# Four schedule edits to a two-block transformer kernel: squares one pair later, rotations by exchanged rows, first squares added by GpSimd, a second bank for odd heads

## The chip, the cores and the metric

One core of one Trainium2 chip runs the whole program in one launch. The metric is the device time of that core in microseconds; the number quoted for a kernel is the median of its runs.

## The reference, cut to what matters

256 tokens of 2048 features pass through two blocks of two layers each, all in float32. The first block has a sparse and a latent attention mixer, each followed by a 4096-wide gated feed-forward; the second has two "hybrid" layers with four groups of four heads (fox, diff, moba, gla).

```python
x = x + rms_norm(mixer(rms_norm(x, g1)), g2)          # layers 0 and 1 of the first block
x = x + rms_norm(channel_mixer(rms_norm(x, g3)), g4)
...
q1, q2, k1, k2 = (partial_rope(t, *rope_diff) for t in (q1, q2, k1, k2))
mq = partial_rope(to_heads(p["moba_q"], HEAD_DIM), *rope_moba)
mk = partial_rope(to_heads(p["moba_k"], HEAD_DIM), *rope_moba)
...
def partial_rope(t, cos, sin):                        # half = 8 rows (diff) or 16 (moba)
    t1, t2, rest = t[..., :half], t[..., half:rot], t[..., rot:]
    return jnp.concatenate([t1 * c - t2 * s, t1 * s + t2 * c, rest], axis=-1)
```

## The kernel before

Features lie on the 128 partitions and tokens along the row, so a tile is 128 x 256 and the state `X` has 16 tiles. The weights stream from HBM in 902 units of eight 128 x 128 blocks (512 KB). SyncE loads a unit into one of four `RING` buffers. ScalarE copies it rounded to fp32r (`high`, L882, into `WHI`), VectorE subtracts to get the remainder (`low`, L1296, into `WLO`), and TensorE multiplies: each block costs three 256-column products, or one of 512 and one of 256 columns in the wide form. A unit's `low` lets SyncE load the next one, and `unit_used` from TensorE frees its `WHI`/`WLO` pair, four deep. Every engine runs its own instruction stream in order and meets the others at semaphores; the four streams are written out from one schedule.

The work beside the weight products (attention heads, rotations, norms, gates) is written as generators. `later(n, part)` starts a part at the n-th unit of a stage, `together` runs several in the order in which they are listed, and each engine advances them by one step for each unit (`tick`). The steps of one engine at one tick follow that tick's `high` or `low`.

A normalised product begins with a `lead`: four outputs are accumulated at once over 16 tiles of `X`, two tiles (a pair) for each unit. For each pair ScalarE writes the rounded `H` tile (`halve`, L897) and the squares (`square`, L889), VectorE writes the remainder (L1306), and TensorE adds the squares over the partitions with a product by a table of ones into bank 7 (`square_sums`, L525). There are five leads. The first waits for the table (`TB`) that ScalarE's queue loads with the inputs; `square` waits until TensorE has read the buffer four tiles back (`sq_read`). In the other four, VectorE first makes the new `X` tile (L1348 and L1350), from the norm of the branch before.

Where an output run ends in a norm, GpSimd adds the squares of 15 tiles (`sums`, L1998 and L2001), and TensorE makes two products: one of that sum (L531) and one of the last square (L533). ScalarE's last square stands behind the `high` copies of that step.

A hybrid layer has 29 tiles of projections (58 units, ticks 0 to 57), values (32 units, ticks 58 to 89) and gates. The rotation of a tile is a TensorE product with a 128 x 128 table (L679, bank 5), three VectorE operations (L1687 to L1689), 16 tiles for each layer, one at a tick from tick 48 and from tick 59. A head passes over its iterations: scores (L830), masks and maxima, exponentials (L1234), normalising (L1885), transposes (L840), the product with the values (L820, L821) into `head_bank`, always bank 7, and VectorE's copy out of it (L1894, `p_head_taken`), which the next head's product waits for. GLA's values product (`gla_heads`, L787 and L789, banks 4 and 5) comes at tick 74 on TensorE; fox's last copy is at tick 73 on VectorE.

Of the kernel before, what the change touches and what calls it, by code (L numbers as in the profile page):

```python
# [14 lines left out]
P = 128  # L15
T = 256
KT = 16
# [4 lines left out]
BANKS = 4  # L22
# [13 lines left out]
       ("moba_cos", 256), ("moba_sin", 256), ("diff_rot", 128), ("moba_rot", 128), ("mla_rot", 128),  # L36
# [49 lines left out]
def program(nc, xT, pos, w, vec, tab, out, n_units):  # L86
# [3 lines left out]
    with ctx:  # L90
# [120 lines left out]
        class Heads:  # L211


            def __init__(self, kind):
# [3 lines left out]
                self.split = kind in ("dsa", "mla")  # L218
                if kind == "mla":
# [41 lines left out]
        def head_bank(h):  # L261
            return BANK[7][:, 0:T]
# [25 lines left out]
        def pooled(k):  # L288
# [13 lines left out]
        ROPE_DIFF, ROPE_MOBA = [[(at + h, f"{kind}_rot", tcol(f"{kind}_cos", T), tcol(f"{kind}_sin", T))  # L302
                                 for at in tiles for h in range(4)]
                                for kind, tiles in (("diff", (Z_DQ, Z_DK)), ("moba", (Z_MQ, Z_MK)))]
# [94 lines left out]
        SUMMED_ADDED = (1, 3, 5, 7, 9, 10)  # L399
# [46 lines left out]
        def _(pe):  # L446
            c = {}
# [70 lines left out]
            def square_sums(tiles):  # L518

                if tiles[0] == 0:  # L520
                    step_no(c, "event")
                    pe.wait_ge(sem("tables"), 16)
# [272 lines left out]
            def heads(kind, l, p0, v0):  # L795
# [15 lines left out]
                for k in range(a.n + 2):  # L811
                    if k >= 2:
# [7 lines left out]
                        mm(head_bank(h), a.value(0, h), p[:, 0:T], start=True, stop=False)  # L820
                        mm(head_bank(h)[:, P:T], a.value(1, h), p[:, T:T + P], start=False, stop=True)\  # L821
# [28 lines left out]
            def hybrid(l):  # L850
# [3 lines left out]
                    later(48, rope(ROPE_DIFF)), later(59, rope(ROPE_MOBA)),  # L854
# [16 lines left out]
        def _(act):  # L871
# [27 lines left out]
            def first_norm():  # L899
# [5 lines left out]
                act.dma_start(TB[:, :], tab).then_inc(sem("tables"), 16)  # L905
                act.dma_start(V[:, KT:], vec[:, KT:]).then_inc(sem("vectors"), 16)
# [13 lines left out]
            def lead(r, u0):  # L920
                (name, l), e = c["lead"], step_no(c, "lead_event") - 1
                x0 = step_no(c, "x_new", KT) - KT if u0 else 0
                for p in range(UB):
# [10 lines left out]
                    for k in (2 * p, 2 * p + 1):  # L934
                        square(k, X[:, k, :], "sq_read", e)
                    if p >= 2:
                        high(u0 + SPLIT + p - 2, 0, 0)
                        tick(c)
                high(u0 + SPLIT + 6, 0, 0)
                tick(c)  # L940
                if u0 == 0:
# [1256 lines left out]
```

## Time and profile before

| | us |
|---|---|
| median of 3 runs | 2869.17 (2868.96 to 2871.13) |
| the profiled execution, time | 2871.13 |
| its span, first to last instruction | 2869.3 |
| TensorE busy | 2775.5 (97%) |
| VectorE busy | 1946.3 (68%) |
| ScalarE busy | 1382.3 (48%) |
| GpSimd busy | 505.5 (18%) |

The profiled execution is 1.96 us above the median of the runs; some 2 us of its time lie outside its span. TensorE's products overlap in the records, so its busy share is not the share of its peak. A wait of another engine counts for the time only where TensorE ends up waiting too.

### The profile page before, as it was taken

Reading aid. Unit: us, or ns where it says so; the run is one execution under the profiler, and the core shown is the slowest. Engines: PE = TensorE matmul, PEld = TensorE weight load, DVE = VectorE, ACT = ScalarE, POOL = GpSimd, SP = SyncE. Lnnn points to the kernel's source line nnn. Section 1 sums busy time; section 2 is a strip of 40 time slices with the busy share of each in tenths; the row PEclk is TensorE's granted clock in tenths of the full one; section 3 lists DMA queues with packets and bytes.
Section 4 is the critical chain, followed back from the end, with each engine's and each line's share of the span. In section 5 each row is a group of like instructions: output and inputs, shape, how many; then the busy total and the mean of one; then the engine's idle time right before and its main releaser. Section 6 shows DMA issues by size and latency. Waiting matters only on the chain.

```text
span 2869.3 us, 50364 instructions
## 1 busy us (share of the span) xinstructions
PE 2775.5 (97%) x18406; PEld 2504.2 (87%) x18406; DVE 1946.3 (68%) x2829; ACT 1382.3 (48%) x1931; POOL 505.5 (18%) x472
## 2 busy tenths in 40 slices
PE   8999999999999999989999999999999999999998
PEld 8998888888888899888888888899878889987887
DVE  4585568777754687668777754586767766676775
ACT  4434555544544447445554543453346454334553
POOL 0060034444411000022444421000000010000001
PEclk9999999999999999999999999999999999999999
DMA  6555445555555454444555555455444555444454
GB/s 226 165 165 184 138 141 181 186 185 185 183 191 184 145 172 156 132 147 147 190 187 184 185 190 184 152 165 162 159 148 150 167 184 169 162 155 153 147 170 139
DMA packets 131914, 481.71 MB, mean 168 GB/s; under 512 B 14768, under 2 KB 14896, under 8 KB 131632
## 3 DMA queue, kind: packets, MB, share of 16 engines
q1 hardware_dynamic: 130608, 475.06, 50.7%
q10 hardware_dynamic: 1152, 4.47, 0.4%
q8 instruction: 112, 1.84, 0.3%
q14 instruction: 42, 0.34, 0.0%
HBM read 477.38 MB, written 2.10 MB: 167 GB/s over the span
## 4 chain that ended last, share of the span: by engine, by line
PE 88%; DVE 6%; ACT 3%; POOL 2%; issue 1%; DMA 1%; ACTq 0%; DVEq 0%; POOLq 0%
PE BANK L458 32%; PE BANK L453 26%; PE BANK L459 16%; PE BANK L474 7%; DVE WLO L1296 2%; ACT WHI L882 1%; PE BANK L525 1%; PE BANK L830 1%; PE BANK L820 1%; PE BANK L465 1%; DMA TB<-tab 1%; PE BANK L679 0%; DVE TM L1885 0%; POOL M L2014 0%; DVE TM L1318 0%
## 5 line engine op out<-in xcount | busy, mean ns | idle before, releaser
L1296 DVE TENSOR_TENSOR WLO<-RING,WHI 128x1024 fp32r<-128x1024 f32 x902 | 1109.5, 1232 | 676.9 <-ACT WHI L882 670.7
L882 ACT ACTIVATE WHI<-RING 128x1024 fp32r<-128x1024 f32 x902 | 953.2, 1058 | 1152.3 <-PE BANK L459 641.1
L458 PE MATMUL BANK<-H,WHI 128*128 128x512 f32 x2560 | 918.7, 403 | 15.1 <-DVE H L1306 10.1
L453 PE MATMUL BANK<-H,WHI 128*128 128x256 f32 x4160 | 772.3, 288 | 22.8 <-DVE H L1306 19.5
L459 PE MATMUL BANK<-H,WLO 128*128 128x256 f32 x2560 | 720.4, 281 | 0.0
L453 PEld LDWEIGHTS BANK<-H,WHI 128*128 128x128 f32 x4160 | 656.8, 193 | 30.6 <-issue 23.8
L458 PEld LDWEIGHTS BANK<-H,WHI 128*128 128x128 f32 x2560 | 483.9, 189 | 136.9 <-issue 16.0
L453 PE MATMUL BANK<-H,WLO 128*128 128x256 f32 x2080 | 591.5, 284 | 0.0
L458 PE MATMUL BANK<-BIGR,WHI 128*128 128x512 f32 x1536 | 541.5, 398 | 3.5 <-DVE BIGR L1913 3.5
L459 PEld LDWEIGHTS BANK<-H,WLO 128*128 128x128 f32 x2560 | 486.2, 190 | 1.7 <-issue 1.0
L459 PE MATMUL BANK<-BIGR,WLO 128*128 128x256 f32 x1536 | 431.1, 281 | 0.0
L453 PEld LDWEIGHTS BANK<-H,WLO 128*128 128x128 f32 x2080 | 402.0, 193 | 0.0
L458 PEld LDWEIGHTS BANK<-BIGR,WHI 128*128 128x128 f32 x1536 | 288.4, 188 | 74.7 <-DVE BIGR L1913 4.2
L459 PEld LDWEIGHTS BANK<-BIGR,WLO 128*128 128x128 f32 x1536 | 290.2, 189 | 0.0
L474 PE MATMUL BANK<-WHI,H 128*128 128x512 f32 x640 | 213.6, 403 | 1.7 <-DVE BIG L1394 1.7
L2001 POOL TENSOR_TENSOR TM<-TM 128x256 f32<-128x256 f32 x84 | 114.3, 1360 | 421.4 <-ACT TM L1000 415.6
L1967 POOL TENSOR_TENSOR TM<-TM,RS 128x256 f32<-128x256 f32 x128 | 116.7, 914 | 361.8 <-DVE TM L1301 360.2
L1998 POOL COPY TM<-TM 128x256 f32<-128x256 f32 x6 | 5.9, 978 | 946.9 <-ACT TM L1000 638.7
L453 PE MATMUL BANK<-BIGR,WHI 128*128 128x256 f32 x688 | 135.2, 295 | 11.5 <-DVE BIGR L1680 4.0
L474 PEld LDWEIGHTS BANK<-WHI,H 128*128 128x128 f32 x640 | 120.2, 188 | 27.4 <-DVE BIG L1394 2.3
L1301 DVE TENSOR_REDUCE TM<-BANK 128x256 f32<-128x512 f32 x128 | 87.8, 690 | 63.1 <-PE BANK L459 63.1
L474 PE MATMUL BANK<-WLO,H 128*128 128x512 f32 x320 | 124.8, 390 | 0.0
(280 smaller groups left out, 2392.5 us busy)
## 6 DMA issues: line engine op xcount, KB each, us to landing
RING<-w SPq DMA_DIRECT2D x902, 512.0 KB, 3.3
X<-xT ACTq DMA_DIRECT2D x4, 512.0 KB, 10.0
TB<-tab ACTq DMA_DIRECT2D x1, 1536.5 KB, 16.7
outT<-M SPq DMA_DIRECT2D x3, 512.0 KB, 2.9
V<-vec ACTq DMA_DIRECT2D x1, 644.0 KB, 19.0
outT<-M SPq DMA_DIRECT2D x2, 256.0 KB, 3.2
BIG<-pos ACTq DMA_DIRECT2D x1, 128.0 KB, 3.9
V<-vec ACTq DMA_DIRECT2D x1, 8.0 KB, 6.9
```

The lines of the kernel that those rows point to most:

```text
L453: last = mm(bank[:, 0:T], wt[s][:, kk, :], x, start=start and n == 0, stop=stop and n == 2)
L458: mm(bank[:, :], WHI[s][:, kk, :], both, start=start, stop=False)
L459: return mm(bank[:, 0:T], WLO[s][:, kk, :], hi, start=False, stop=stop)
L465: last = mm(pair[t][:, 0:T], x[:, t * P:(t + 1) * P], wt[s][:, kk:kk + 2, :].rearrange("p a b -> p (a b)"), start=start and n == 0, stop=s ...
L474: last = mm(pair[t][:, :], x[:, t * P:(t + 1) * P], wt[s][:, kk:kk + 4, :].rearrange("p a b -> p (a b)"), start=start and n == 0, stop=sto ...
L525: last = mm(BANK[7][:, 0:T], ones, TM[:, k % 4, :], start=k == 0, stop=k == KT - 1)
L820: mm(head_bank(h), a.value(0, h), p[:, 0:T], start=True, stop=False)
L882: A(WHI[at % SPLIT][:, :, :], RING[at % RAW][:, :].rearrange("p (k n) -> p k n", k=UB), ACT.Copy)\
L1296: TT(WLO[at % SPLIT][:, :, :], RING[at % RAW][:, :].rearrange("p (k n) -> p k n", k=UB), WHI[at % SPLIT][:, :, :].bitcast(f32), ALU.subtra ...
L1301: return v.tensor_reduce(dst, bank[:, :].rearrange("p (a t) -> p t a", a=2), AX.X, ALU.add)
L1967: g.tensor_tensor(y, y, RS[:, :], ALU.mult).then_inc(sem("y_scaled"), 1)
L2001: g.tensor_tensor(TM[:, 4, :], TM[:, 4, :], TM[:, k % 4, :], ALU.add).then_inc(sem("sq_added"), 1)
```

## The change

1. In every lead, ScalarE squares the pair before the one that it has just halved, and the last pair after the loop. VectorE moves the remainder of tile k-1 between the two operations that make tile k of `X`.
2. In the first lead TensorE makes no product of single squares; GpSimd adds them (`sums`), and TensorE makes two products at the lead's end. The first 384 columns of the table go out after the second quarter of `X`; the rest, with the parameters, goes out at the fifth pair, and ScalarE and VectorE wait for them at the end of that run.
3. At the last step of a run that ends in a norm, the square goes ahead of the last `high`.
4. Rotations use no product: twelve transfers for each hybrid layer copy the partner rows of four tiles at once into `TM[8:12]` (four for each of the two diff turns, two for each of the two moba turns), and VectorE makes three operations of 1024 columns for four tiles, one at a tick. The sign has gone into the sine table, and two 128-column tables are gone.
5. Odd heads of dsa, mla and fox use bank 5, so that a head waits for the copy of the head before the last. GLA's values product waits for fox's four copies.

```diff
+    self.banks = 2 if kind in ("dsa", "mla", "fox") else 1
-        def head_bank(h):
-            return BANK[7][:, 0:T]
+        def head_bank(a, h):
+            return BANK[5 if a.banks == 2 and h % 2 else 7][:, 0:T]
...
-        SUMMED_ADDED = (1, 3, 5, 7, 9, 10)
+        SUMMED_ADDED = (0, 1, 3, 5, 7, 9, 10)
... TensorE, lead
-                    if h:
+                    if h and u0:
                         square_sums((2 * h - 2, 2 * h - 1))
-                square_sums((KT - 2, KT - 1))
+                if u0:
+                    square_sums((KT - 2, KT - 1))
+                else:
+                    pe.wait_ge(sem("ones"), 16)
+                    sums()
... TensorE, gla_heads and heads
+                pe.wait_ge(sem("p_head_taken"), HEADS_1 + 12 * l + 4)
-                        if h0 + h >= 1:
-                            pe.wait_ge(sem("p_head_taken"), h0 + h)
+                        free = h0 + h + 1 - (a.banks if h else 1)
+                        if free:
+                            pe.wait_ge(sem("p_head_taken"), free)
... TensorE, hybrid
-                    later(48, rope(ROPE_DIFF)), later(59, rope(ROPE_MOBA)),
... ScalarE, lead
-                    for k in (2 * p, 2 * p + 1):
-                        square(k, X[:, k, :], "sq_read", e)
+                    for k in (2 * p - 2, 2 * p - 1) if p else ():
+                        square(k, X[:, k, :], taken, e)
+                    if u0 == 0 and p == 4:
+                        act.dma_start(TB[:, TO["chunk"]:], tab[:, TO["chunk"]:]).then_inc(sem("tables"), 16)
+                        act.dma_start(V[:, KT:], vec[:, KT:]).then_inc(sem("vectors"), 16)
... ScalarE, the last step of a run that ends in a norm
-                    early = upo if r.kind in ("m", "add") or taps_led else upo - 1
+                    ends = r.tail and isinstance(i, int) and i * BANKS + j == r.n - 1
+                    early = upo if r.kind in ("m", "add") and not ends or taps_led else upo - 1
... ScalarE, hybrid: swap at ticks 44, 53, 60, 68
+            def swap(l, n, o0):
+                kind, at = TURNS[n]
+                act.wait_ge(sem("bank_free"), o0 + at + 4)
+                if n or l:
+                    act.wait_ge(sem("roped"), len(MLA_ROPE) + 16 * l + 4 * n)
+                for src, dst, rows in TURN_ROWS[kind]:
+                    act.dma_start(SWAPPED[dst:dst + rows], BIG[src:src + rows, at:at + 4, :]).then_inc(sem("swapped"), 16)
+                yield
... VectorE, lead
-                            then(STT(TM[:, 8 + k % 2, :], M[:, k, :], vcol(post[0], KT * post[1] + k), TM[:, 10, :],
-                                     ALU.mult, ALU.mult))
-                            TT(X[:, k, :], X[:, k, :], TM[:, 8 + k % 2, :], ALU.add).then_inc(sem("x_new"), 1)
+                            STT(TM[:, 8 + k % 2, :], M[:, k, :], vcol(post[0], KT * post[1] + k), TM[:, 10, :],
+                                ALU.mult, ALU.mult).then_inc(sem("dve_step"), 1)
                             if k:
                                 halve(k - 1, pre, pl)
+                            dve.wait_ge(sem("dve_step"), step_no(c, "dve_step"))
+                            TT(X[:, k, :], X[:, k, :], TM[:, 8 + k % 2, :], ALU.add).then_inc(sem("x_new"), 1)
... VectorE, hybrid: turn at ticks 47, 56, 63, 71, listed ahead of the heads
+            def turn(l, n):
+                kind, at = TURNS[n]
+                x = BIG[:, at:at + 4, :]
+                dve.wait_ge(sem("swapped"), 16 * step_no(c, "swapped", len(TURN_ROWS[kind])))
+                TT(SWAPPED, SWAPPED, across(f"{kind}_sin"), ALU.mult).then_inc(sem("turn"), 1)
+                yield
+                TT(x, x, across(f"{kind}_cos"), ALU.mult).then_inc(sem("turn"), 1)
+                yield
+                dve.wait_ge(sem("turn"), step_no(c, "turn", 2))
+                TT(x, x, SWAPPED, ALU.add).then_inc(sem("roped"), 4)
+                yield
```

## Rows read from the trace of the kernel before

**Rows 1.** The page, busy time of each engine and its share of the span
```profile
PE 2775.5 (97%) x18406; PEld 2504.2 (87%) x18406; DVE 1946.3 (68%) x2829; ACT 1382.3 (48%) x1931; POOL 505.5 (18%) x472
```

**Rows 2.** Waits of TensorE: us in total, times, longest; last row from 2200 to 2250
```profile
PE BANK L820 <- DVE BIG L1894: 16.8, 20, 3.3
...
PE BANK L679 <- DVE TM L1687: 0.9, 2, 0.4
...
PE BANK L820 <- DVE BIG L1894: 3.9, 2, 3.3
```

**Rows 3.** Timeline of TensorE in the first lead: start, us, line, operation, idle before
```profile
14.64 0.35 PE L453 MATMUL BANK<-H,WHI 128*128 128x256 f32 x1
...
20.34 0.48 PE L525 MATMUL BANK<-TM,TB 128*128 128x256 f32 x1 [2.61 <-DMA TB<-tab]
...
45.88 0.59 PE L453 MATMUL BANK<-H,WHI 128*128 128x256 f32 x2
```

**Rows 4.** Windows: busy PE, PEld, DVE, ACT, POOL, granted clock, DMA share, GB/s
```profile
21.60:24.80 3.20, 3.20 (x17) 3.20 (x17) 1.50 (x3) 2.07 (x4) 0.00 (x0) 0.50 0.63 252
2223.20:2225.50 2.30, 2.30 (x8) 2.03 (x9) 2.30 (x2) 0.92 (x1) 0.00 (x0) 0.50 0.71 224
```

**Rows 5.** The chain in order of time: two units of projections, two of values
```profile
2039.05 5.76 PE BANK L453 x48
2099.10 5.48 PE BANK L474 x24
```

**Rows 6.** Timeline of GpSimd: one addition of squares in a busy stretch, one in an idle
```profile
952.55 1.47 POOL L2001 TENSOR_TENSOR TM<-TM 128x256 f32<-128x256 f32 x1 [9.54 <-ACT TM L1000]
2851.97 0.73 POOL L2001 TENSOR_TENSOR TM<-TM 128x256 f32<-128x256 f32 x1 [4.15 <-ACT TM L1000]
```

**Rows 7.** Timeline of TensorE: two rotations in a row, a unit between them
```profile
2025.25 0.60 PE L679 MATMUL BANK<-BIG,TB 128*128 128x256 f32 x2
2028.55 0.60 PE L679 MATMUL BANK<-BIG,TB 128*128 128x256 f32 x2
```

**Rows 8.** Timeline of a dsa head: the copy out and the next head's product
```profile
304.76 0.42 DVE L1894 COPY BIG<-BANK 128x256 f32<-128x256 f32 x1
305.32 0.67 PE L820 MATMUL BANK<-TM,BIG 128*128 128x256 f32 x2 [0.57 <-DVE BIG L1894]
```

**Rows 9.** Timeline around GLA's values product: VectorE at tick 73, TensorE at 74
```profile
2104.21 1.23 DVE L1296 TENSOR_TENSOR WLO<-RING,WHI 128x1024 fp32r<-128x1024 f32 x1 [3.39 <-ACT WHI L882]
2104.42 0.59 PE L787 MATMUL BANK<-BIG 128*128 128x256 f32 x2
2105.35 0.42 DVE L1894 COPY BIG<-BANK 128x256 f32<-128x256 f32 x1
```

**Rows 10.** Timeline of VectorE where the projections end, tick 56
```profile
2043.11 1.23 DVE L1296 TENSOR_TENSOR WLO<-RING,WHI 128x1024 fp32r<-128x1024 f32 x1 [0.95 <-ACT WHI L882]
2044.90 0.42 DVE L1394 TENSOR_TENSOR BIG<-BANK,RS 128x256 f32<-128x256 f32 x1 [0.56 <-PE BANK L453]
```

**Rows 11.** Timeline of two run ends: VectorE's evacuation, ScalarE's copy and last square
```profile
401.28 0.42 DVE L1428 TENSOR_TENSOR M<-M,BANK 128x256 f32<-128x256 f32 x1 [0.49 <-PE BANK L453]
402.30 0.40 ACT L1000 ACTIVATE TM<-M 128x256 f32<-128x256 f32 x1
...
962.34 0.69 DVE L1301 TENSOR_REDUCE M<-BANK 128x256 f32<-128x512 f32 x1 [0.44 <-PE BANK L459]
963.36 0.40 ACT L1000 ACTIVATE TM<-M 128x256 f32<-128x256 f32 x1
```

**Rows 12.** Timeline of a later lead's first tile: ScalarE's rounding, VectorE's remainder
```profile
968.22 0.51 ACT L897 ACTIVATE H<-X,V 128x256 fp32r<-128x256 f32 x1 [2.80 <-DVE X L1350]
968.96 0.48 DVE L1306 SCALAR_TENSOR_TENSOR H<-X,V,H 128x256 fp32r<-128x256 f32 x1
```

**Rows 13.** DMA issues of the page: KB each, us to landing
```profile
TB<-tab ACTq DMA_DIRECT2D x1, 1536.5 KB, 16.7
...
BIG<-pos ACTq DMA_DIRECT2D x1, 128.0 KB, 3.9
```

More of the change, by code:

```diff
@@ L301, in program, with across @@
         MLA_ROPE = [(k, "mla_rot", big(CD_COS), big(CD_SIN)) for k in (CD_KR, CD_QR, CD_QR + 1, CD_QR + 2, CD_QR + 3)]
-        ROPE_DIFF, ROPE_MOBA = [[(at + h, f"{kind}_rot", tcol(f"{kind}_cos", T), tcol(f"{kind}_sin", T))
-                                 for at in tiles for h in range(4)]
-                                for kind, tiles in (("diff", (Z_DQ, Z_DK)), ("moba", (Z_MQ, Z_MK)))]
+        TURNS = (("diff", Z_DQ), ("diff", Z_DK), ("moba", Z_MQ), ("moba", Z_MK))
+        TURN_ROWS = {"diff": [(0, 8, 8), (8, 0, 8), (64, 72, 8), (72, 64, 8)], "moba": [(0, 16, 16), (16, 0, 16)]}
+        SWAPPED = TM[:, 8:12, :]
+        def across(table):
+            return tcol(table, T).rearrange("p (a t) -> p a t", a=1).broadcast_to([P, 4, T])
         GROUPS = ("gla", "fox", "diff", "moba")
@@ L521, in square_sums @@
                     step_no(c, "event")
-                    pe.wait_ge(sem("tables"), 16)
                 for k in tiles:
@@ L904, in first_norm @@
                         act.dma_start(V[:, 0:KT], vec[:, 0:KT]).then_inc(sem("gains"), 16)
-                act.dma_start(TB[:, :], tab).then_inc(sem("tables"), 16)
-                act.dma_start(V[:, KT:], vec[:, KT:]).then_inc(sem("vectors"), 16)
+                    if quarter == 1:
+                        act.dma_start(TB[:, :TO["chunk"]], tab[:, :TO["chunk"]]).then_inc(sem("ones"), 16)
                 c["lead"], c["scale"] = ("mix_pre", 0), True
@@ L920, in lead @@
             def lead(r, u0):
-                (name, l), e = c["lead"], step_no(c, "lead_event") - 1
+                name, l = c["lead"]
+                taken = "sq_read" if u0 else "sq_added"
+                e = step_no(c, "lead_event" if u0 else "added") - 1
                 x0 = step_no(c, "x_new", KT) - KT if u0 else 0
@@ L938, in lead @@
                         tick(c)
+                for k in (KT - 2, KT - 1):
+                    square(k, X[:, k, :], taken, e)
                 high(u0 + SPLIT + 6, 0, 0)
                 tick(c)
-                if u0 == 0:
-                    act.wait_ge(sem("tables"), 16)
-                    act.wait_ge(sem("vectors"), 16)
                 scale()
@@ L1027, in run @@
                 groups(act, c, r, step, beside and beside(l, o0), led)
+                if u0 == 0:
+                    act.wait_ge(sem("tables"), 16)
+                    act.wait_ge(sem("vectors"), 16)
                 if r.kind == "ffn":
@@ L1043, in short @@
                         step_no(c, "short_out")
+                    if early and m == r.n - 1:
+                        leave(m, BANK[(o0 + m) % BANKS])
                     if m == r.last(m) and r.ends_unit(m):
@@ L1046, in short @@
                         tick(c)
-                    if early:
+                    if early and m < r.n - 1:
                         leave(m, BANK[(o0 + m) % BANKS])
@@ L1264, in hybrid @@
                     later(10, gla_levels(l, o0)), later(37, log_gates(l)),
+                    *(later(at, swap(l, n, o0)) for n, at in enumerate((44, 53, 60, 68))),
                     later(62, heads("fox", l)), later(76, gla_heads(l)), later(78, heads("diff", l)),
@@ L1893, in heads @@
                         dve.wait_ge(sem("p_head_done"), h0 + k - 1)
-                        v.tensor_copy(a.out(k - 2), head_bank(k - 2)).then_inc(sem("p_head_taken"), 1)
+                        v.tensor_copy(a.out(k - 2), head_bank(a, k - 2)).then_inc(sem("p_head_taken"), 1)
                     if a.split and k >= 3:
@@ L1919, in hybrid @@
                     later(10, gla_levels(l)), later(36, log_gates(l)),
-                    later(48, rope(ROPE_DIFF)), later(59, rope(ROPE_MOBA)),
+                    *(later(at, turn(l, n)) for n, at in enumerate((47, 56, 63, 71))),
                     later(62, heads("fox", l)), later(75, gla_heads(l)), later(78, heads("diff", l)),
@@ L2042, in _ @@
             schedule(Engine(
-                first_norm=nothing, run=run, index=nothing, windows=windows, pool=nothing, attend=nothing, attended=nothing,
+                first_norm=sums, run=run, index=nothing, windows=windows, pool=nothing, attend=nothing, attended=nothing,
                 post_norm=nothing, mixer_cd=nothing, queries=nothing, lru=nothing, first_heads=nothing,
@@ L2097, in rope_tables @@
             rows = slice(at + half * rot // 2, at + (half + 1) * rot // 2)
-            cos[rows], sin[rows] = np.cos(ang).T, np.sin(ang).T
+            cos[rows], sin[rows] = np.cos(ang).T, (1 if half else -1) * np.sin(ang).T
     return cos, sin
@@ L2111, in tables @@
     t["moba_cos"], t["moba_sin"] = rope_tables(128, 32, 500000.0)
-    t["diff_rot"], t["moba_rot"], t["mla_rot"] = turn(8, 64), turn(16, 128), turn(32, 64)
+    t["mla_rot"] = turn(32, 64)
     t["freq"] = (10000.0 ** (-(np.arange(P) % 32) / 32.0))[:, None]
```

9 lines of the change are left out of this document (6 added, 3 removed).

## The prediction

> **What bounds the kernel now.** I read the page first: TensorE is busy 97% of the span, the next engine 68% [rows 1]. So a microsecond counts only if it comes out of TensorE's own stream or out of one of its waits, and everything taken off VectorE or ScalarE alone is worth nothing. The second view is the list of TensorE's waits. The edits touch three of its entries: the products of heads wait 16.8 us in 20 waits for the copy of the head before, the rotations wait 0.9 us, and the first lead waits 2.6 us for the table [rows 2, 3]. The rest of the sum has to come from work that TensorE no longer does. So the third view is the timeline, for the price of one such product on TensorE: not its own duration, which overlaps its neighbours, but how much further apart the units stand.
>
> **First lead.** TensorE finishes unit 0 at 14.64, and the lead ends, squares included, at 45.88 [rows 3]: 31.2 us for seven more units. A unit without extras is 5.76 / 2 = 2.88 us [rows 5]; seven are 20.2. What the rest holds: the wait of 2.61 us for the table [rows 3]; the granted clock of 0.50 from 21.60 to 24.80 (1.2 instead of 2.4 GHz), in which 3.2 us do the work of 1.6 [rows 4]; the 16 ones-products and small handoffs. GpSimd takes over the adding, and TensorE keeps two products, 0.84 us at the 0.42 found below for a rotation's, which has the same shape. If nothing else paces the lead it ends at 14.64 + 20.2 + 0.84 = 35.7: a gain of 10.2. The table's 2.6 us wait goes with its consequence, the low clock behind it, because TensorE no longer stands still there.
>
> What can pace it instead is GpSimd: each square now waits until the tile four back is added. One addition took 0.73 us with VectorE idle and 1.47 us while a `low` ran beside it [rows 6]. With 1.47 for both additions of a pair and 0.05 for each handoff, a pair takes 3.04, which is 0.16 above TensorE's 2.88, or 1.1 us over seven pairs. I take that: gain 9.1. The lower bound: if VectorE and GpSimd excluded each other wholly, a pair would need 2 x 0.73 + 2 x 0.48 + 1.23 = 3.65 us [rows 6, 9, 12], 0.77 over, so 5.4 us: gain 4.8. The Trainium skill speaks for this bound: by SBUF — State Buffer, § Who interferes with whom, a VectorE instruction with two SBUF inputs and a GpSimd instruction that reads SBUF shut each other out for their whole length. By that rule the opening gains 4.8 instead of 9.1; the trace agrees in that an addition doubles beside a `low`, but has no stretch where both are full.
>
> The late table and parameters (about 2 MB at the fifth pair) are two issues on ScalarE's queue, about 1 us. ScalarE is then more than one pair ahead of TensorE, and a unit's load has three units to land; the first readers come after the run, some 30 us later. I cost them at nothing; if that cover were gone, it would be their 1 us and a late unit or so, inside the range.
>
> **Rotations.** In the projections two rotations start 2028.55 - 2025.25 = 3.30 us apart with one unit between [rows 7], against 2.88 without: 0.42 us each. Sixteen for each layer and two layers make 32 x 0.42 = 13.4 us, and the 0.9 us of waits go too: 14.3. The half of them that stand in the values stage have the shorter unit of 5.48 / 2 = 2.74 [rows 5]; I use the same price there. Bound below: 0.30, half its duration of 0.60 [rows 7], so 9.6 instead of 13.4.
>
> In their place ScalarE issues 12 transfers a layer, four at once in the worst tick. At half a microsecond each that is 2 us beside the 1.06 us copy in a tick of 2.88, and ScalarE is 48% busy [rows 1] and its copy is wanted two units later. VectorE waits for the transfers three ticks after their issue, 3 x 2.88 = 8.6 us. Nearest rows: a 128 KB load lands in 3.9 us, the 1.5 MB table in 16.7 [rows 13]; these are 32 or 64 KB, so I take the first and no wait. VectorE does three operations of 1024 columns for four tiles, 1.23 us each by the operation of the same shape [rows 9], in place of twelve short ones: less work, but in lumps of 1.23 at a tick.
>
> Two lumps fall where TensorE is waiting for VectorE. The second turn starts at tick 56, between the `low` at 2043.11 and the evacuation of the last projection at 2044.90, which had 0.56 us of idle time before it [rows 10]. 1.23 - 0.6 puts the evacuation 0.6 later, and the first values product waits for it: 0.6 in each layer, a loss of 1.2. The other is below.
>
> **Heads.** Waits of 0.57 us like the one at 305.32 [rows 8] vanish where a head has two banks: product h then needs only the copy of head h - 2. What TensorE wants next (the turned probabilities, the next scores' mask) is done earlier on both engines. Of the 16.8 us, moba keeps its own, 3.9 in the first hybrid layer and about as much in the second [rows 2]; 16.8 - 7.9 = 8.9 us go. The scores, masks and copies are the same.
>
> **GLA's new wait.** GLA uses bank 5 and now waits for fox's last copy. TensorE arrives at 2104.42; the copy on VectorE begins at 2105.35 and ends at 2105.77 [rows 9], so even alone it is 1.35 us late, and the handoff takes 0.14 (305.18 to 305.32) [rows 8]. But tick 73 is also the last step of the fourth turn, and turns are listed ahead of heads: the 1024-column addition slips in before the copy, which ends at about 2107.0. The wait is 2.7 us, twice 5.4. Behind it stand the whole values product and the weights. Idle times near this length were followed by half clock: 2.61 us before 20.34, then 0.50 from 21.60 to 24.80, and again 0.50 from 2223.20 to 2225.50 after the 3.3 us wait in moba [rows 2, 3, 4]. Half of 2.3 to 3.2 us is 1.15 to 1.6 lost; I take 1.2 in each layer. Together a loss of 5.4 + 2.4 = 7.8. Bounds: nothing (if VectorE ran ahead of where it runs now) to 8.6.
>
> **Run ends and later leads.** The last square at 402.30 could start at 401.74, when the evacuation is done (401.28 + 0.42, and 0.04); that at 963.36 could start at 963.07 [rows 11]. TensorE stands idle behind both. Two ends of either kind: 2 x 0.56 + 2 x 0.29 = 1.7. The last run has no copy there, so it gains nothing. In the four later leads the first remainder could start at 968.22 + 0.51 + 0.04 = 968.77 instead of 968.96 [rows 12]: 4 x 0.19 = 0.7. VectorE's cycle then runs through ScalarE: addition, rounding, remainder, so a pair costs about 3.7 us, as against TensorE's 2.88 plus 0.84 for two ones-products. That is even, and the slow first unit gives both a start; the later squares cost nothing and loosen ScalarE. I count nothing more, with 2 us of loss as bound.
>
> **Sum.** Gains 9.1 + 14.3 + 8.9 + 1.7 + 0.7 = 34.7; losses 1.2 + 7.8 = 9.0; net 25.7. The profiled execution goes from 2871.1 to 2845.4; it lies 2.0 above the median, so against the median 2869.2 - 25.7 = 2843.5.
>
> **Rivals.**
> 1. GLA does not wait, or waits so little that the clock stays: losses of 0 to 3 instead of 7.8, so 2836 to 2838. For it: VectorE's streams shift when rotations leave TensorE. Against: VectorE's tick 73 hangs on ScalarE's evacuation of the values, which TensorE itself releases. 15%.
> 2. The opening is paced by the port that VectorE and GpSimd share: gain 4.8 there, 2847.8; with a loss in the later leads 2850. 14%.
> 3. The other side: the exchanged rows come late. VectorE stands at the turn, its `low` copies behind it, and TensorE runs dry. The cover is 8.6 us plus about two units of converted weights, 5.7. From a landing of 14.3 us on it costs, eight times; at 14.3 + 25.7 / 8 = 17.5 us the whole gain is gone, at 19 us the time would be 2881. Only the 1.5 MB table took as long as 16.7 [rows 13], and these are fifty times smaller. 4%.
> 4. Some wait that I don't see eats the gain: 2869 or a little more. 5%, half of it within the bound.
>
> **How the numbers follow.** The forecast has 62%, with its own range 2839 to 2848 from the bounds of the clock, of the rotations and of GpSimd. With rivals 1 and 2 the range is 2835 to 2852. No change can be told below about 0.2%, 5.7 us. Faster: 62 + 15 + 14 = 91%; within 0.2%: 3%; slower: 4 + 2 = 6%.
>
> **What the profile after would show.** The first lead ends near 37 us, without a wait for a table and at full clock from its first unit on; L679 is left with the five tiles of the first block; L820's waits are down to moba's four; L787 has a new wait of 2.7 us behind L1894 in each hybrid layer, and the windows after it show clock 0.5; the first L474 of each layer waits 1.2 us; the squares at run ends start 0.3 to 0.6 us earlier. The forecast is wrong if L787 does not wait, if additions on GpSimd stretch the first lead beyond 39 us, or if the turn's first operation on VectorE waits for a transfer.

## The result, and the profile after

The changed kernel takes 2832.15 us (median of four executions, 2819.42 to 2837.55) beside 2869.12 before (four, 2868.96 to 2871.13): a ratio of 0.987, with a 95% interval of 0.9836 to 0.9904. Timed again on another chip it took 2833.5 beside 2862.5 (six and 29 executions), ratio 0.9877 [0.9843, 0.9911]. The forecast was 2843.5 with a range from 2835 to 2852: the direction was right, the gain larger than the range allowed.

The profiled execution after is the slowest of the four: 2837.55 us, span 2835.7. Beside the one of before (2871.13, span 2869.3) that is 33.6 us less, where 25.7 were forecast. So the miss of 11.3 us is made of 7.9 us of terms and of 5.4 us between the profiled execution after and its median, less the 2.0 by which the one of before lay above its own. The experiments had to explain both.

The page's busy times of the changed kernel, to be read beside [rows 1]:

```profile
PE 2749.1 (97%) x18314; PEld 2484.2 (88%) x18314; DVE 1945.8 (69%) x2757; ACT 1379.4 (49%) x1931; POOL 518.3 (18%) x487
```

TensorE's waits after (in total, times, longest), to be read beside [rows 2]:

```profile
PE BANK L457 <- DVE H L1334: 19.0, 3, 9.2
PE BANK L462 <- DVE H L1334: 9.8, 2, 4.9
PE BANK L829 <- DVE BIG L1938: 8.0, 4, 3.3
PE BANK L795 <- issue: 4.8, 2, 2.4
...
PE BANK L462 <- DVE WLO L1324: 3.3, 2, 1.6
PE BANK L540 <- ACT TM L1013: 2.8, 3, 1.0
PE BANK L478 <- DVE BIG L1423: 2.6, 3, 1.1
```

The head products (now L829) wait for a copy only four times, in moba, where they waited 20 times; a wait of 0.6 us at fox's first head, with no releaser named, is new in each layer. L795 is GLA's new wait, 2.4 us in each hybrid layer. The list names no releaser ("issue"); the timeline further down shows fox's last copy ending just before it. The weights' own wait L462, 1.6 us twice, is in both kernels, and becomes important below.

The end of the first lead after, with TensorE's only two ones-products in it (L538 and L540):

```profile
33.82 0.28 PE L457 MATMUL BANK<-H,WLO 128*128 128x256 f32 x1
33.94 0.59 PE L538 MATMUL BANK<-TM,TB 128*128 128x256 f32 x2
34.37 0.59 PE L540 MATMUL BANK<-TM,TB 128*128 128x256 f32 x2
34.62 0.59 PE L457 MATMUL BANK<-H,WHI 128*128 128x256 f32 x2
```

The groups of GpSimd and VectorE from 12 to 40 us: count, then busy time and mean ns of one.

```profile
L2045 POOL TENSOR_TENSOR TM<-TM 128x256 f32<-128x256 f32 x14 | 12.7, 908 | 6.2 <-ACT TM L897 4.9
...
L1324 DVE TENSOR_TENSOR WLO<-RING,WHI 128x1024 fp32r<-128x1024 f32 x10 | 13.6, 1380 | 0.1
L1334 DVE SCALAR_TENSOR_TENSOR H<-X,V,H 128x256 fp32r<-128x256 f32 x14 | 11.7, 877 | 0.5 <-ACT H L905 0.5
```

The two engines' operations last longer beside each other: a remainder (L1334) takes 877 ns on average here, and 0.48 us in the kernel before [rows 12]. But TensorE has no wait in this stretch, and the granted clock stays at 2.4 GHz. Windows of the changed kernel (PE, PEld, DVE, ACT, POOL busy, then the clock) over the first lead and over GLA's products, beside [rows 4]:

```profile
12.00:40.00 28.00, 28.00 (x229) 27.90 (x229) 26.94 (x30) 21.42 (x41) 13.11 (x15) 1.00 0.81 301
...
2073.00:2081.00 8.00, 7.36 (x30) 6.26 (x31) 1.67 (x3) 0.00 (x0) 0.00 (x0) 0.79 0.38 131
```

GLA's products (TensorE L795), the turn's addition (L1734) and fox's last copy (L1938), beside [rows 9]:

```profile
2071.98 1.22 DVE L1734 TENSOR_TENSOR BIG<-BIG,TM 128x1024 f32<-128x1024 f32 x1
2073.12 0.42 DVE L1938 COPY BIG<-BANK 128x256 f32<-128x256 f32 x1
2073.64 0.67 PE L795 MATMUL BANK<-BIG 128*128 128x256 f32 x2 [2.42 <-issue]
```

The order is the forecast one: addition, copy, product. So is the new lump at the end of the projections, beside [rows 10]: the turn's first operation in front of the evacuation, and the first values product waiting for it.

```profile
2015.30 1.22 DVE L1729 TENSOR_TENSOR TM<-TM,TB 128x1024 f32<-128x1024 f32 x1
2016.44 0.42 DVE L1423 TENSOR_TENSOR BIG<-BANK,RS 128x256 f32<-128x256 f32 x1
2016.91 0.50 PE L478 MATMUL BANK<-WHI,H 128*128 128x512 f32 x1 [1.06 <-DVE BIG L1423]
```

**Where the time went, stage by stage.** TensorE signals the end of each unit of weights (`unit_used`), so two traces can be laid beside each other, signal by signal. The table gives how much longer (+) or shorter (-) a stretch between two signals, counted from 0, lasts than in the kernel before, in us. The kernels with one part of the change alone are those of the experiments.

| units | what runs there | changed | opening alone | rotations alone | banks alone | squares alone | before, once more |
|---|---|---|---|---|---|---|---|
| to 0 | first unit | -0.9 | -0.1 | -1.2 | -0.9 | -0.2 | -1.0 |
| 0-9 | first lead | -10.4 | -10.1 | +2.0 | +2.1 | +0.1 | +0.6 |
| 80-118 | dsa heads | -5.0 | 0 | 0 | -5.1 | 0 | 0 |
| 118-134 | second lead | -1.4 | +0.2 | +0.3 | -0.7 | -0.5 | -0.7 |
| 134-311 | first FFN | 0 | 0 | 0 | -9.4 | 0 | -9.4 |
| 311-321 | third lead | -0.8 | +0.1 | -0.1 | +0.7 | -0.1 | +0.7 |
| 321-366 | | -0.8 | +0.1 | 0 | -1.1 | +0.1 | -1.1 |
| 366-400 | mla heads | -4.7 | 0 | 0 | -3.9 | +0.1 | +0.9 |
| 400-416 | fourth lead | -1.1 | -0.2 | -0.3 | -0.9 | -0.1 | +0.1 |
| 416-592 | second FFN | 0 | -9.4 | +0.1 | +0.1 | 0 | -9.4 |
| 592-602 | fifth lead | -0.6 | +1.2 | +0.1 | 0 | -0.2 | +0.1 |
| 640-661 | rotations, layer 1 | -6.3 | +0.2 | -6.3 | 0 | 0 | 0 |
| 661-670 | fox, GLA, layer 1 | +2.9 | 0 | +1.1 | +0.1 | -0.1 | 0 |
| 670-760 | | 0 | +1.1 | +1.0 | -0.1 | -0.5 | +1.1 |
| 795-815 | rotations, layer 2 | -6.3 | 0 | -6.3 | 0 | 0 | 0 |
| 815-824 | fox, GLA, layer 2 | +2.9 | 0 | +1.1 | +0.1 | 0 | 0 |
| 824-902 | to the end | -1.1 | -1.1 | -1.2 | -1.1 | +0.5 | -1.6 |

The last column is the unchanged kernel in another execution, and shows what is no part of any change: steps of about 1 us at the leads and the last stretch, and two steps of 9.4 us in the FFNs.

Many of the small steps follow the granted clock. In stretch 321-366 TensorE waits 3.5 us for VectorE in every trace, and then runs at half clock (1.2 GHz) for a longer or a shorter time, or not at all. Nine microseconds from the start of the unit with that wait, in the kernel before, in the changed kernel and in the one of experiment 2 with fox in one bank (TensorE, its weight loads, VectorE, ScalarE, GpSimd, then the clock):

```profile
1067.50:1076.50 9.00, 5.53 (x27) 5.51 (x27) 4.96 (x11) 1.44 (x2) 0.00 (x0) 0.62 0.56 177
1049.10:1058.10 9.00, 5.50 (x33) 5.50 (x34) 4.97 (x11) 2.47 (x4) 0.00 (x0) 0.81 0.59 177
1049.60:1058.60 9.00, 5.44 (x46) 5.42 (x46) 5.86 (x12) 3.19 (x6) 0.00 (x0) 1.00 0.55 177
```

That unit lasts 8.94, 8.00 and 6.70 us, and the stretch differs by 0, -0.8 and -2.3. The fourth lead goes the same way (a clock of 0.57 over 12 us before, 0.72 in the changed kernel), and so does the +2.0 of two kernels in the first lead, which also wait 3.3 and 3.5 us for the table instead of 2.6. Not every step has this cause: the changed kernel's -0.9 up to signal 0 does not.

### The profile page after: what moved, and what is told of

Same layout as the page of the kernel before. It is cut to its first block, busy times and chain, and to the rows that moved or that the text cites. A ratio compares the mean times of both kernels' runs of the same rounds, so it can differ in the third digit from the quotient of the medians.

```text
span 2835.7 us, 50169 instructions
## 1 busy us (share of the span) xinstructions
PE 2749.1 (97%) x18314; PEld 2484.2 (88%) x18314; DVE 1945.8 (69%) x2757; ACT 1379.4 (49%) x1931; POOL 518.3 (18%) x487
## 4 chain that ended last, share of the span: by engine, by line
PE 90%; DVE 5%; ACT 2%; POOL 2%; issue 1%; DMA 0%; DVEq 0%; ACTq 0%; POOLq 0%
PE BANK L462 32%; PE BANK L457 28%; PE BANK L463 16%; PE BANK L478 8%; DVE WLO L1324 1%; PE BANK L839 1%; PE BANK L532 1%; ACT WHI L890 1%; PE BANK L469 1%; PE BANK L829 1%; PE BANK L849 0%; POOL M L2058 0%; DVE TM L1346 0%; PE BANK L676 0%; POOL M L2061 0%
## 5 line engine op out<-in xcount | busy, mean ns | idle before, releaser
L462 PE MATMUL BANK<-H,WHI 128*128 128x512 f32 x2560 | 917.8, 403 | 14.7 <-DVE H L1334 9.8
L462 PEld LDWEIGHTS BANK<-H,WHI 128*128 128x128 f32 x2560 | 483.0, 189 | 136.0 <-issue 15.3
L462 PE MATMUL BANK<-BIGR,WHI 128*128 128x512 f32 x1536 | 539.9, 396 | 3.4 <-DVE BIGR L1957 3.4
L462 PEld LDWEIGHTS BANK<-BIGR,WHI 128*128 128x128 f32 x1536 | 288.2, 188 | 73.4 <-DVE BIGR L1957 4.1
L2045 POOL TENSOR_TENSOR TM<-TM 128x256 f32<-128x256 f32 x98 | 127.0, 1296 | 426.0 <-ACT TM L1013 414.0
```

The costliest lines, as they stand in the source:

```text
L462: mm(bank[:, :], WHI[s][:, kk, :], both, start=start, stop=False)
L2045: g.tensor_tensor(TM[:, 4, :], TM[:, 4, :], TM[:, k % 4, :], ALU.add).then_inc(sem("sq_added"), 1)
```

## The experiments

**1. The change once more, and its four parts alone.** Each against the kernel before on the same chip; the first four ran on one chip, the squares on another. The edits are the parts of the change's own diff; in the kernel with the opening alone, the squares stay beside their own pair.

> The changed kernel itself, timed once more. If its spread of 18 us belongs to the kernel, five more rounds scatter again between about 2819 and 2838 us, with a median near 2831; if it was an accident of that chip, they lie within 3 us of each other, as those of the kernel before do. Prediction as on record: 2843.5 us.

Measured: 2833.54 median (2817.64 to 2842.89, six executions); the kernel before on the same chip 2862.51 (2849.07 to 2874.32, 29 executions). The scatter is no property of the change: the kernel before has it too, 25 us wide. That its first four executions lay within 2.2 us of each other, near 2870, I take for luck: the changed kernel scattered by 18 us beside them. That something kept only the kernel before at the slow end there is not excluded.

```
-                square_sums((KT - 2, KT - 1))
+                if u0:
+                    square_sums((KT - 2, KT - 1))
+                else:
+                    pe.wait_ge(sem("ones"), 16)
+                    sums()
...
-                first_norm=nothing, run=run, index=nothing, windows=windows, pool=nothing, attend=nothing, attended=nothing,
+                first_norm=sums, run=run, index=nothing, windows=windows, pool=nothing, attend=nothing, attended=nothing,
```

> Only the opening: GpSimd adds the first squares, TensorE does two ones-products in place of sixteen, tables go out later; squares stay beside their own pair. By the terms on record: 9.1 us less, 2860.1. By the alignment of the two traces: 11.3 us less, 2858. By the rival with the shared port: 4.8 us less, 2864.4. If the scatter of the changed kernel comes from the opening (loads, GpSimd), the runs here spread by over 5 us; otherwise by 2 to 3.

Measured: ratio 0.9954 [0.993, 0.9977], median 2853.15. In the trace the first lead is 10.1 us shorter: the 10.2 of an unpaced lead, not 9.1, and not the rival's 4.8. TensorE's wait for the table and the half clock behind it are both gone. In the middle of the lead each unit takes 2.88 us instead of 3.73, which is the two ones-products, 0.43 each, and nothing else.

```
-                    later(48, rope(ROPE_DIFF)), later(59, rope(ROPE_MOBA)),
+                    *(later(at, turn(l, n)) for n, at in enumerate((47, 56, 63, 71))),
```

> Only the rotations: exchanged rows by DMA and three VectorE operations in place of sixteen products on TensorE in each layer. By the terms on record: 14.3 us less and 1.2 more at the two projection ends, 13.1 us less, 2856.1, since GLA has no new wait here. By the alignment of the two traces (0.42 for each in the projections, 0.45 in the values, 0.5 lost at each end) about 13 us less too. If exchanged rows come late in some executions, the scatter of the changed kernel shows here (over 5 us); otherwise 2 to 3 us.

Measured: ratio 0.9962 [0.994, 0.9983], median 2855.11 (mean 2854.1 beside 2864.2). In the trace 6.3 us go in each layer, 12.6 in both, the loss at the end of the projections included; 13.1 was the term. No turn waits for a transfer. New is 1.1 us in each layer at fox. The fourth turn's first operation (L1709) stands ahead of the copy of fox's third head (L1918), and fox's last product (L823), which in the kernel before did not wait at all, waits 0.95 us for that copy. VectorE and TensorE in this kernel:

```profile
2092.18 1.22 DVE L1709 TENSOR_TENSOR TM<-TM,TB 128x1024 f32<-128x1024 f32 x1
2093.31 0.42 DVE L1918 COPY BIG<-BANK 128x256 f32<-128x256 f32 x1
2093.87 0.67 PE L823 MATMUL BANK<-TM,BIG 128*128 128x256 f32 x2 [0.95 <-DVE BIG L1918]
```

```
-            return BANK[7][:, 0:T]
+            return BANK[5 if a.banks == 2 and h % 2 else 7][:, 0:T]
```

> Only the second bank for odd heads, with GLA's wait for fox's last copy. By the terms on record: waits of 8.9 us less; GLA waits for a copy that isn't behind the turn's addition, 1.35 + 0.14 = 1.5 us in each layer and perhaps 1.2 for the clock: net 3.5 to 5.9 us less, 2863 to 2866. By the alignment of the two traces each removed wait gives 0.7 to 0.8 instead of 0.47 to 0.57: 12.5 less, 3 to 5 more: net 7.5 to 9.5 us less, 2860 to 2862. If the scatter comes from the heads or from GLA's wait and its clock, it shows here.

Measured: ratio 0.9958 [0.9941, 0.9974], median 2853.08 (mean 2853.2 beside 2864.2). In the trace 5.0 at dsa, 4.8 at mla (unit by unit; a step of 0.9 in the stretch belongs to no change) and 1.42 in each layer at fox go, 12.6 together; GLA's new wait takes 1.55 in each layer. The same head as [rows 8], without the copy in its way (TensorE alone):

```profile
304.73 0.28 PE L454 MATMUL BANK<-BIGR,WLO 128*128 128x256 f32 x1
304.86 0.60 PE L823 MATMUL BANK<-TM,BIG 128*128 128x256 f32 x2
305.29 0.38 PE L824 MATMUL BANK<-TM,BIG 128*128 128x128 f32 x2
305.51 0.82 PE L833 MATMUL BANK<-BIG 128*128 128x128 f32 x4
305.98 0.59 PE L454 MATMUL BANK<-BIGR,WHI 128*128 128x256 f32 x2
```

And TensorE in the kernel before, around the line of [rows 8]:

```profile
304.48 0.28 PE L453 MATMUL BANK<-BIGR,WLO 128*128 128x256 f32 x1
...
305.83 0.39 PE L821 MATMUL BANK<-TM,BIG 128*128 128x128 f32 x2
306.05 0.82 PE L830 MATMUL BANK<-BIG 128*128 128x128 f32 x4
306.52 0.47 PE L453 MATMUL BANK<-BIGR,WHI 128*128 128x256 f32 x1
```

The wait shown is 0.57 us. But from the start of the last weights product to the start of the next it is 306.52 - 304.48 = 2.04 before and 305.98 - 304.73 = 1.25 without the wait: 0.79. The shown idle time begins at the end of a product of 0.28, while a product that needn't wait starts 0.13 after the last one's start; and the two products behind the wait start 0.51 apart (305.32 to 305.83) instead of 0.43. 0.15 + 0.08 = 0.23 us of a wait are not in its bracket. Fox's waits of 0.47 gave 0.71 each by the same sum, GLA's of 1.3 costs 1.55, and its 2.42 in the changed kernel costs 2.65 where the clock holds.

```
-                    for k in (2 * p, 2 * p + 1):
+                    for k in (2 * p - 2, 2 * p - 1) if p else ():
                         square(k, X[:, k, :], "sq_read", e)
```

> Only the squares one pair later in the four later leads, VectorE's remainder ahead of the addition there, and the evacuation's square ahead of the next weights at run ends. By the terms on record: 1.7 + 0.7 = 2.4 us less. By the alignment of the two traces the starts of the four later leads gained 1.5, 0.8, 1.2 and 0.6 us: 4.0 less. Rival on record: VectorE's cycle now runs through ScalarE and costs up to 2 us. In the traces at equal pace of the two large runs; the means scatter by 2 us.

Measured: ratio 1.0002 [0.9979, 1.0026] on a second chip. In the trace the four later leads together are 0.9 us shorter; in two traces of the changed kernel they are 3.9 shorter, in a third 1.4, and in the second trace of the kernel before they differ by 0.2 in sum and 0.7 singly. But most of that spread is the clock. The 3.9 belong to traces in which the fourth lead's half clock was the shorter one, and the kernel with the banks alone, which has none of this part, gains 0.9 there in the same way. Only two traces with this part have half clock for as long as the kernel before in all four leads: this one, 0.9 shorter, and the third of the changed kernel, 1.4. So this part is worth about 1 us, with one step of 0.7 that no change explains; its term had been 2.4.

**2. GLA's wait.**

```
-                self.banks = 2 if kind in ("dsa", "mla", "fox") else 1
+                self.banks = 2 if kind in ("dsa", "mla") else 1
-                pe.wait_ge(sem("p_head_taken"), HEADS_1 + 12 * l + 4)
```

> The changed kernel with fox's heads back in one bank, and so without GLA's wait. By the terms on record fox gives back 2 x 2 waits of about 0.47 us, and GLA's 7.8 us go: 5.9 less than the changed kernel. By the traces: 4 x 0.71 = 2.8 given back, 8.7 saved, but the turn's addition still stands ahead of fox's last copies (1.14 in each layer, in the kernel with the rotations alone): 3.6 less. Rival: the wait is GLA's own and moves elsewhere: nothing gained.

Measured: ratio 0.9893 [0.9868, 0.9918]. In the trace each layer loses 0.71 + 0.70 at fox's first heads and 1.19 at the last (the wait behind the turn's first operation again, not behind its addition as expected), and gains 4.36 at GLA: 1.8 a layer, 3.5 in both beside the trace of the changed kernel.

```
-                    later(62, heads("fox", l, o0 + 13, o0 + 33)), later(74, gla_heads(l, o0 + 29)),
+                    later(62, heads("fox", l, o0 + 13, o0 + 33)), later(75, gla_heads(l, o0 + 29)),
-                for _ in range(3):
+                for _ in range(2):
```

> The changed kernel with TensorE's GLA products one unit later. If GLA's wait is lateness of the copy alone (2.4 us against a unit of 2.74), the wait and the half clock after it go and nothing comes in their place: 8.7 us less than the changed kernel in the trace (4.36 in each layer), 7.8 by the terms on record. Rival: VectorE's copies of GLA's output and the three units that follow have no slack, and 1 to 3 us in each layer return there.

Measured: ratio 0.987 [0.9846, 0.9894], mean 2822.4; the changed kernel's was 2831.2 on another chip. In the trace 4.36 us go in each layer, all of it. The same window as for the changed kernel:

```profile
2073.00:2081.00 8.00, 8.00 (x41) 6.87 (x40) 4.83 (x9) 2.77 (x3) 0.00 (x0) 1.00 0.61 196
```

TensorE is never idle and the clock is 1.00 instead of 0.79. So the copy was late by less than a unit, and in the stretch of the wait nothing came in its place. Further on, stretch 670-760 is 2.6 us longer than in the changed kernel's first trace; it is so in that kernel's third trace too, with the wait in place, so the edit need not be its cause.

**3. The steps of 9.4 us.** In all traces TensorE's units last 2.773 us up to unit 132 of the first FFN. There it waits 1.6 us for VectorE, and from then on until the FFN ends every unit lasts 2.827 us on average, or every one 2.773. Windows of 40 us in each of the two FFNs (TensorE's busy time and products come first), in the kernel before (the profiled execution, then the second one) and in the kernel with the opening alone:

```profile
600.00:640.00 40.00, 40.00 (x229) 34.72 (x228) 29.03 (x36) 19.56 (x24) 17.54 (x18) 1.00 0.57 187
1450.00:1490.00 40.00, 40.00 (x228) 34.64 (x227) 29.64 (x37) 19.58 (x25) 16.46 (x16) 1.00 0.57 187
```

```profile
600.00:640.00 40.00, 40.00 (x232) 35.24 (x231) 29.56 (x36) 21.17 (x27) 17.90 (x18) 1.00 0.57 184
1450.00:1490.00 40.00, 40.00 (x233) 35.28 (x232) 29.98 (x36) 20.86 (x26) 17.27 (x17) 1.00 0.57 186
```

```profile
600.00:640.00 40.00, 40.00 (x228) 34.71 (x228) 29.48 (x36) 19.97 (x26) 18.76 (x19) 1.00 0.57 184
1450.00:1490.00 40.00, 40.00 (x233) 34.99 (x232) 29.87 (x36) 20.93 (x26) 17.37 (x17) 1.00 0.57 186
```

TensorE is fully busy in all of them, at the same granted clock; three to five more products fit, or they don't. 177 units by 0.053 are the 9.4 us. The first execution has both FFNs at the slower pace, the second both at the faster, the third one of each.

```
-                    if r.kind == "ffn" and j % 2 == 0:
+                    if led and r.kind == "ffn" and isinstance(i, int) and (i, j) == (1, 1):
+                        gelu(1, -1)
+                    if r.kind == "ffn" and j % 2 == 0 and not taps_led:
```

> The changed kernel with one ScalarE instruction moved in each of the two large runs: the second gelu goes behind the next rounding of weights. In all six traces TensorE's unit lasts 2.773 us up to that point; there it waits 1.6 to 1.9 us for VectorE, and from there to the end of the run each of some 176 units lasts either 2.827 (ten of twelve runs) or 2.773 us (the second run in the kernel with the opening alone, the first in the kernel with the banks alone). Theory: this wait is where the pace is drawn, and it is the scatter of all kernels of this case, before and after: steps of 176 x 0.053 = 9.4 us. Then without the wait the pace stays at 2.773: 3.8 us less from the two waits and 18.8 less than the profiled execution of the changed kernel, about 2815 us in nearly all executions, spread under 6 us. Rival 1: the wait goes but the pace is drawn elsewhere: median 2827, spread 20 us. Rival 2: the wait comes back a unit later: nothing changes.

Measured: ratio 0.9886 [0.9854, 0.9919]; the six executions are 2815.9, 2816.4, 2818.2, 2826.1, 2837.3 and 2838.0. Of the wait of 1.63 us two small ones are left (the second 0.36 in the bracket). The two units around the wait are 1.7 us shorter and the one behind them 0.2 longer: 1.5 in each FFN, 3.0 in both. But the pace is drawn as before, slow in the first FFN of its trace and fast in the second. That is rival 1: a short wait draws it as well as a long one.

```
+                        again = r.kind == "ffn" and not isinstance(i, int) and j == 0 and h == 1
-                        pe.wait_ge(sem("lo_done"), i * (BANKS * upo) + (at + 1))
+                        pe.wait_ge(sem("lo_done"), i * (BANKS * upo) + (at + (3 if again else 1)))
```

> The changed kernel with a short wait of TensorE added in each of the 14 loop turns of the first large run of either FFN: at the second unit of a turn it waits for the weights of two units later, which by the trace are ready about 0.4 us after it arrives. Theory (a wait of TensorE draws the pace anew): within one trace the units between two such waits last 2.773 us in some turns and 2.827 us in others, and the time no longer falls into three groups 10 us apart. The waits cost 2 x 14 x 0.4 = 11 us, and the mix of paces gives back some of it. Rival (the pace is set once at the start of the run, or by the other engines): all units of a run keep one pace between the waits, and only the cost shows.

Measured: 2861.73 median, ratio 0.9974 [0.9959, 0.9989], and ten executions within 11.3 us (2853.6 to 2864.9), not in three groups. In the trace the pace is constant between two waits, and where it changes, it changes at one. The first FFN's turns from unit 137 to 248 run at 2.773, 2.827, 2.827, 2.827, 2.773, 2.773, 2.827, 2.773, 2.773, 2.827, 2.773, 2.773, 2.827, 2.773. TensorE's products in a fast turn (count, busy, mean ns):

```profile
L462 PE MATMUL BANK<-H,WHI 128*128 128x512 f32 x57 | 20.0, 395 | 0.4 <-DVE WLO L1325 0.4
L463 PE MATMUL BANK<-H,WLO 128*128 128x256 f32 x56 | 15.5, 277 | 0.0
```

and in a slow one, two turns later:

```profile
L462 PE MATMUL BANK<-H,WHI 128*128 128x512 f32 x52 | 18.4, 399 | 0.0
L463 PE MATMUL BANK<-H,WLO 128*128 128x256 f32 x52 | 14.6, 281 | 0.0
```

The wait at the edge of such a turn:

```profile
638.38 0.28 PE L463 MATMUL BANK<-H,WLO 128*128 128x256 f32 x1
639.07 0.50 PE L462 MATMUL BANK<-H,WHI 128*128 128x512 f32 x1 [0.41 <-DVE WLO L1325]
```

So a wait of TensorE draws the pace of the back-to-back products that follow, and they keep it until the next wait. The rival, a pace set once for the whole run, falls. Not every stretch is drawn, though: the five units ahead of the first wait take 2.773 us in both FFNs of all 14 traces. The cost was expected too low. An added wait makes its unit mostly 0.6 to 0.7 us longer, not 0.4 (the bracket's 0.41 and some 0.23 that no bracket shows), and the first one 5.2 us in the first FFN and 4.9 in the second. There VectorE is still behind, so TensorE waits 3.3 us, and half clock follows, as at GLA. The eight microseconds around it in the first FFN:

```profile
449.70:457.70 8.00, 4.66 (x18) 4.02 (x18) 4.40 (x5) 1.66 (x3) 1.80 (x3) 0.79 0.71 237
```

> The kernel before, once more, for its trace: if the time follows the pace, an execution near 2870 shows 2.827 us for the units of both FFNs, one near 2860 shows 2.773 us in one of them, and one near 2850 in both. If the pace and the time are unrelated, any pair can occur.

> The changed kernel, once more, for its trace: near 2838 us both FFNs at 2.827 us a unit, near 2829 one at 2.773, near 2819 both.

Measured: the kernel before 2851.44 us, both FFNs at 2.773; the changed kernel 2842.14, both at 2.827. Both fit. The changed kernel's time is 4.6 above its other two executions at this pace. Beside the first trace GLA costs 3.3 less here, and the steps elsewhere 8.0 more, 2.6 of them in stretch 670-760.

**4. The edits that shortened the trace, together.**

> The changed kernel with both edits that paid alone: TensorE's GLA products one unit later and the second gelu behind the next rounding of weights. If they add up in the trace at equal pace: 6.1 to 8.7 and 3.4 us, so 9.5 to 12 us less than the changed kernel; executions near 2827, 2818 and 2808 us by the number of FFNs at the slower pace, mean about 2820. Rival: the two share a cover and give only the larger.

Measured: ratio 0.9844 [0.9816, 0.9871], six executions from 2813.65 to 2832.43, mean 2822.5. In the trace GLA gives 4.3 in each layer and the gelu 1.5 in each FFN, 11.7, as alone; some 3.4 us of the steps elsewhere go the other way. The mean is that of the kernel with GLA alone (2822.4, six executions), so the times can't tell the second edit from nothing; the trace can. Both kernels are faster than the kernel before. That they are faster than the changed kernel, whose ratio is 0.9877 [0.9843, 0.9911], is shown by the traces alone.

## Why the prediction was wrong in size

Two steps failed. The term of 8.9 us for the heads was the sum of idle times, and the waits were worth 12.5. And the time of 2869.2, from which the 25.7 were taken off, was treated as the kernel's own to within 0.2%, while one kernel's executions lie up to 25 us apart. The terms, with what the two profiled executions showed:

| term | predicted | the two profiled executions |
|---|---|---|
| opening | -9.1 (4.8 to 10.2) | -10.4 |
| rotations less the projection ends | -13.1 | -12.6 |
| heads of dsa, mla, fox | -8.9 | -12.5 |
| run ends and later leads | -2.4 | -3.9 (elsewhere -0.9, -1.4) |
| GLA's wait with the clock | +7.8 | +8.6 (elsewhere +5.3, +7.0) |
| steps that belong to no change | 0 | -2.8 |
| sum | -25.7 | -33.6 |

**Heads: the term that was sized wrongly.** The prediction took "8.9 us go" from the list of waits, that is, idle time in brackets. Sixteen waits were worth 0.23 us more each: 3.7 us, nearly half of the missing 7.9. The prediction had priced a rotation by how much further apart the units stand, and that came out right (12.6 for 13.1); it did not do the same for the waits, though fox in the kernel before would have shown it: a unit with a wait of 0.47 lasts 4.14 us there, and the one of the last head, which does not wait, 3.46.

**Opening.** The mechanism was right, the pacing by GpSimd was not. With 0.73 for an addition and the durations of the remainder and `low`, a pair is 3.65 us of work for VectorE and GpSimd together. In the trace of the changed kernel VectorE began its pairs at 19.95, 23.40, 26.30 and 29.20, so three pairs took 9.25 us instead of 10.95, and GpSimd began six additions in that time. VectorE's rows of the second and third interval:

```profile
26.30 1.85 DVE L1334 SCALAR_TENSOR_TENSOR H<-X,V,H 128x256 fp32r<-128x256 f32 x2
28.07 1.21 DVE L1324 TENSOR_TENSOR WLO<-RING,WHI 128x1024 fp32r<-128x1024 f32 x1
29.20 1.91 DVE L1334 SCALAR_TENSOR_TENSOR H<-X,V,H 128x256 fp32r<-128x256 f32 x2
```

So the two don't exclude each other wholly, though operations of both last longer side by side. By the Trainium skill, SBUF — State Buffer, § Who interferes with whom, they should; this trace agrees in the stretched durations and not in the whole length. The rival that rested on it (2847.8, 14%) did not come true. GpSimd stood idle between additions, waiting for squares (4.9 us in five waits), so it did not set the pace; and VectorE's 9.25 us beside the 8.64 of three units on TensorE never reached TensorE, which has no wait in this stretch.

**GLA.** Place, order and releaser were right. The wait was 2.42 instead of 2.7 us and cost 2.65. The clock's part was put at 1.2 and is not one number: 1.7 us in both layers of the profiled execution (4.36 - 2.65; the window above at 0.79), in one layer of the second trace of the changed kernel and of the kernel with added waits, and nothing in either layer of the changed kernel's third trace or of the kernel with the gelu later, behind the same wait. Rival 1's idea that the clock stays came true in some executions, but not its reason, a short wait. That the term came out near its 7.8 is in part luck: the wait was shorter than forecast, and the clock cost more where it fell.

**Rotations, projection ends.** Right within 0.5 us. The exchanged rows never came late. What no term had: with one bank, the fourth turn's first operation, ahead of fox's third copy, costs 1.1 us a layer; the second bank hides it in the changed kernel.

**Run ends and later leads.** The 3.9 flatter it: at equal half clock the part gives 0.9 and 1.4 where 2.4 was forecast, and in the time it makes no difference that can be measured.

**The median: the step that was left out.** Of the four executions before, all show the time of the slow pace in both FFNs; two of the four after do (2833.6 and 2837.6), one lies near the time of one fast FFN (2830.7) and one near that of two (2819.4). That attribution is by time, since only profiled executions have a trace. The prediction said that a change below 0.2% couldn't be told; the kernel's own scatter is 25 us, 0.9%. In the traces with both FFNs at the slow pace the changed kernel took 2837.6, 2837.7 and 2842.1, which lies within the range of 2835 to 2852, and below the 2843.5. The median of 2832.15 lies outside because some executions drew the fast pace; the time before stood near the top of its distribution, and the range had no term for that.

## What to carry to other kernels

The bracket of a wait is not its price. Measure how far apart the work on either side stands with and without it; here 0.23 us came on top of each wait on TensorE, which matters when the waits are many and short.

Where a kernel has long stretches without a wait on TensorE, time it often before believing a spread: four executions within 0.1% did not show that the same kernel also runs 20 us faster. Lay two traces of one kernel beside each other, unit by unit, before reading anything from two kernels.

A reused bank brings a wait for its last reader. Ask whether the product can come one unit later: here, in the trace, that gave back what the bank had cost, and the clock with it.

## What was not expected of the hardware

Back-to-back pairs of products of 512 and 256 columns on TensorE go at one of two paces, 0.3533 or 0.3467 us a pair, at a granted clock of 1.00 in both. The pace can change at a wait, of 0.4 or of 1.6 us alike, and is held until the next, over as many as 177 units. Why, what decides the draw, and why the units ahead of the first wait were at the fast pace every time, stays open; whether a kernel with no wait at all there would hold the fast pace of the units before it wasn't reached, since moving the gelu left two short waits.

A new wait of 2.42 us on TensorE was followed by half clock in some executions and not in others, and behind one of 3.5 us the half clock was long, short or absent. Much of the steps of about 1 us between traces is that.
